# Up projections of a transformer layer computed in sets of four blocks by seven quarter products

## The reference

```python
# first layer, D_FF = 4096
h = rms_norm(x, norm_mlp[layer])
x = x + jnp.square(jax.nn.relu(h @ w_up[layer])) @ w_down[layer]

# two layers, two feed-forward parts each, D_FF_2 = 2816
def swiglu(h, w_gate, w_up, w_down):
    return (jax.nn.silu(h @ w_gate) * (h @ w_up)) @ w_down
mod = (c_act @ w_ada[l] + b_ada[l]).reshape(B, N_MOD, D_MODEL)
h = modulate(rms_norm_2(x, norm_gain[l, 0]), mod[:, 0], mod[:, 1])
x = x + 0.5 * mod[:, 2][:, None, :] * swiglu(h, ffn_w_gate[l, 0], ffn_w_up[l, 0], ffn_w_down[l, 0])
```

## Time and profile before

| | us |
|---|---|
| median of 3 runs | 3502.74 (3502.47 to 3504.43) |
| span of the profiled execution | 3498.8 |
| TensorE busy | 3407.7 (97%) |
| GpSimd busy | 2369.8 (68%) |
| VectorE busy | 1179.6 (34%) |
| ScalarE busy | 885.8 (25%) |

### The profile page before, as it was taken

How to read it: one execution, slowest core, us unless ns; L and a number is a source line. 1 busy time by engine, 2 the same in 40 slices (tenths; PEclk the granted TensorE clock), 3 DMA queues, 4 the chain that set the end, 5 groups by cost and what they waited for, 6 DMA issues and landing times.

```text
span 3498.8 us, 42521 instructions
## 1 busy us (share of the span) xinstructions
PE 3407.7 (97%) x17034; PEld 2738.7 (78%) x17034; DVE 1179.6 (34%) x2514; ACT 885.8 (25%) x1876; POOL 2369.8 (68%) x1242
## 2 busy tenths in 40 slices
PE   8888999999999999999999999999999999999999
PEld 6655777988898888667779888888887677798887
DVE  6554332433443234442223111332244422241111
ACT  2656551211120102354312000210012543221000
POOL 7515447787778776645677877687775546678775
PEclk9999999999999999999999999999999999999999
DMA  3222213444535442212232222254432122223222
GB/s 142 68 69 82 67 62 108 149 171 170 185 127 204 168 166 94 73 58 85 85 106 96 97 97 96 83 220 165 171 126 73 67 76 79 82 97 106 98 98 73
DMA packets 104773, 388.09 MB, mean 111 GB/s; under 512 B 12017, under 2 KB 12401, under 8 KB 98433
## 3 DMA queue, kind: packets, MB, share of 16 engines
q1 hardware_dynamic: 88272, 292.76, 24.4%
q10 hardware_dynamic: 16304, 92.62, 7.0%
HBM read 383.20 MB, written 2.13 MB: 110 GB/s over the span
## 4 chain that ended last, share of the span: by engine, by line
PE 92%; DVE 4%; ACT 3%; issue 1%; ACTq 0%; DVEq 0%
PE psum L1234 28%; PE psum L1236 27%; PE psum L1235 27%; PE psum L1307 2%; PE psum L1349 2%; PE psum L1324 2%; PE psum L1293 1%; DVE rs_t L1695 1%; ACT s_sb L1477 0%; DVE s_sb L1736 0%; ACT L1477 0%; ACT s_sb L1495 0%; PE psum L1407 0%; PE psum L1285 0%; DVE n_sum L1906 0%
## 5 line engine op out<-in xcount | busy, mean ns | idle before, releaser
L1202 POOL TENSOR_TENSOR w_hi<-raw,ones 128x1024 fp32r<-128x1024 f32 (+2 forms) x593 | 1041.3, 1756 | 990.4 <-PE psum L1236 981.2
L1205 POOL TENSOR_TENSOR w_lo<-raw,w_hi 128x1024 fp32r<-128x1024 f32 (+2 forms) x593 | 1315.1, 2218 | 46.5
L1234 PE MATMUL psum<-h_hi,w_hi 128*128 128x512 f32 (+2 forms) x2912 | 1143.4, 393 | 19.4 <-DVE r L1711 9.4
L1236 PE MATMUL psum<-h_hi,w_lo 128*128 128x512 f32 (+2 forms) x2912 | 1105.3, 380 | 0.0
L1235 PE MATMUL psum<-h_lo,w_hi 128*128 128x512 f32 (+2 forms) x2912 | 1104.8, 379 | 0.0
L1234 PEld LDWEIGHTS psum<-h_hi,w_hi 128*128 128x128 f32 (+1 forms) x2912 | 550.2, 189 | 156.6 <-issue 35.9
L1236 PEld LDWEIGHTS psum<-h_hi,w_lo 128*128 128x128 f32 (+1 forms) x2912 | 549.7, 189 | 106.6
L1235 PEld LDWEIGHTS psum<-h_lo,w_hi 128*128 128x128 f32 (+1 forms) x2912 | 550.9, 189 | 103.3 <-issue 9.0
L1234 PE MATMUL psum<-a_hi,w_hi 128*128 128x512 f32 (+1 forms) x1064 | 392.5, 369 | 0.0
L1235 PE MATMUL psum<-a_lo,w_hi 128*128 128x512 f32 (+1 forms) x1064 | 391.8, 368 | 0.0
L1236 PE MATMUL psum<-a_hi,w_lo 128*128 128x512 f32 (+1 forms) x1064 | 391.8, 368 | 0.0
(11 more groups left out here) (198 smaller groups left out, 3299.5 us busy)
## 6 DMA issues: line engine op xcount, KB each, us to landing
raw<-weights_dram SPq DMA_DIRECT2D x487, 512.0 KB, 3.3
ada_t<-ada_dram ACTq DMA_DIRECT2D x48, 1536.0 KB, 7.1
raw<-weights_dram SPq DMA_DIRECT2D x76, 256.0 KB, 2.6
raw<-weights_dram SPq DMA_DIRECT2D x32, 384.0 KB, 2.9
bias_t<-biases_dram ACTq DMA_DIRECT2D x36, 256.0 KB, 2.9
bias_t<-cum_dram ACTq DMA_DIRECT2D x16, 256.0 KB, 3.9
out_dram<-x SPq DMA_DIRECT2D x8, 256.0 KB, 2.1
raw<-weights_dram SPq DMA_DIRECT2D x4, 408.0 KB, 3.1
```

Of the source, the lines that this page charges most:

```text
L1202: nc.gpsimd.tensor_tensor(high, piece, ones[:, 0:1].to_broadcast([P, n]), ALU.mult)\
L1205: nc.gpsimd.tensor_tensor(w_lo[:, p % NR, 0:n], piece, high.bitcast(F32), ALU.subtract)\
L1234: mm(dst, lh, rh, start=first, stop=False)
L1236: return mm(dst, ll, rh, start=False, stop=last)
```

## The change

`ffn` and `mlp` no longer make all gates and ups as groups. The first four groups after each norm stay as they were (before it was three that were interleaved with the norm). All others come in sets of four groups, made by `new_set`: two pairs, "g" and "u" (for a feed-forward part two gate blocks and the two up blocks that belong to them; for the MLP four blocks). A pair is a product of 256 output features x 1024 features x 512 tokens. Each matrix is cut into 2x2 quarters, and the pair is made of seven quarter products P1 to P7 in place of eight, with sums of weight quarters and of activation quarters as operands. A quarter product is 4 chunks x 3 passes = 12 matmuls of 256 columns. The two pairs take turns: P1g, P1u, P2g, P2u, P6g, P6u, P5g, P5u, P7g, P7u, P4g, P4u, P3g, P3u. There are 47 sets: 7 in the MLP (1, 2, 2, 2 in its four parts) and 10 in each of the four feed-forward parts (3, 4, 3).

What comes with it:

- Operands. Each of the 14 products has its own place in the ring of six: half of the place is the high part, made by ACT as a copy of 128x512 (L1690), the other half is the low part, by GpSimd, for P3 by VectorE (L1995).
- Weight sums on VectorE, 8 per set, 128x512, SBUF to SBUF (L2006, L2008, L2009 are `first_sums`; L2017 is `last_sum`).
- Result sums. ACT copies P1, P6 and P5 out of PSUM (`keep`, L1701); VectorE adds (`combine`, L2024, L2028, L2033), 6 of 128x256 per set.
- Activation sums per norm: `quarter_sum` (4 instructions of 128x256), a high part on ACT and a low part on VectorE (128x1024, L1990) for each of 4 chunks. The normed value goes to SBUF (`n_out`) rather than to PSUM.
- Adaptation sums: 72 loads of 2 x 1024 columns, and c lies in SBUF (`c_t`) rather than in PSUM.

```diff
-ADA = 3
+ADA = 2
+SET_BANKS = (((0, 1), (2, 3)), ((6, 7), (5, 4)))
+PRODUCTS = ("P1", "P2", "P6", "P5", "P7", "P4", "P3")
...
+def with_operands():
...
+        while place < len(RING) and (place < NH or place - NH in free):
+            one = RING[place]
...
+            yield "operand", one
...
+    for what in PRODUCTS:
+        for p in pairs:
+            put("product", p.ops[what])
+            if what == "P1":
+                p.p1 = tick("copied")
+                put("keep", p, "P1")
+            elif what == "P2":
+                p.c11 = tick("combined")
+                put("c11", p)
...
+            elif what == "P3":
+                p.c12 = tick("combined")
+                put("c12", p)
+                result(p, 0)
...
+            def product(op):
+                pair, what, m = op.pair, op.what, op.pair.norm
+                E.wait_at(op.low)
...
+                elif what == "P6":
+                    E.wait_ge("copied", pair.p1)
+                elif what == "P5":
+                    E.wait_ge("combined", pair.c11)
...
+                    mm(dst, wh[:, w], hi, start=start, stop=False, skip_group_check=True)
+                    mm(dst, wh[:, w], lo, start=False, stop=False, skip_group_check=True)
+                    ins = mm(dst, wl[:, w], hi, start=False, stop=stop, skip_group_check=True)
+                ins.then_inc(sem["product_done"], 1)
...
+            def operand(op):
+                if op.low[0] == "low_dve":
+                    operand_low(op)
+                gate, up = SETS[op.pair.made // 8]
+                if (op.what, op.pair.side) == ("P2", 1):
+                    first_sums(gate)
+                elif (op.what, op.pair.side) == ("P6", 0):
+                    first_sums(up)
+                elif (op.what, op.pair.side) == ("P6", 1):
+                    last_sum(gate)
+                elif (op.what, op.pair.side) == ("P5", 0):
+                    last_sum(up)
...
-                    ins = v.tensor_tensor_reduce(out=part, in0=part, in1=c_bcast, scale=1.0, scalar=0.0, op0=ALU.mult,
+                    ins = v.tensor_tensor_reduce(out=part, in0=part, in1=c_t[:], scale=1.0, scalar=0.0, op0=ALU.mult,
```

429 lines of the change are left out of this document (359 added, 70 removed).

## The result

The changed kernel takes 3793.91 us (median of 4 runs, 3792.62 to 3797.42) against 3502.6 us for the kernel before (4 runs): ratio 1.0832, 95% interval [1.0817, 1.0848]. It is slower by 291 us. The forecast was 3640 and the range ended at 3720, so the sign was right and the size was not: the sum said +140, the profiled spans say 3795.6 - 3498.8 = +297.

A forecast was written before the change was run, and what follows sets the result against it. It took TensorE, busy for 97% of the span, as the bound; -76 + 1.5 + 73 + 48 + 40 + 44 + 10 = +140 us on the 3498.8 us span, with 3.9 around it, gave 3640 us, range 3560 to 3720.

The forecast's parts named there:

- TensorE's own work: All 47 sets: 168 matmuls of 256 columns take 20.2 us where 96 of 512 took 21.8; -76 us.
- From set to set: Feed-forward transitions with a set behind a set: 28 stalls of 2.6 us before P6g, +73 us (0 to 112).
- the walk: Step-by-step timing of one feed-forward transition: P6g waits for the P1g copy, at 28.5 rather than 25.9 us.
- the turns with GpSimd: VectorE's instructions with two SBUF inputs and GpSimd's exclude each other; without turns the transition walk ends at 25.8, no stall.
- Downs with sums: 51 downs carrying an adaptation sum: each loses 0.65 us once GpSimd's 2.7 us lead is gone; +10 us (0 to 33).
- The cycle: In downs with a sum, GpSimd's 4.3 us and two instructions' 2.4, in turns, take about 6.1 us against TensorE's 5.44.
- a first set behind downs finds operands and engines ready: Sets right behind downs: costed at nothing, as are last sets in front of downs.
- Adaptation sums in transitions: Feed-forward transitions holding adaptation sums: the P1g copy comes 3.5 us later per load; two layers +48 us (30 to 70).
- MLP: The MLP's 3 transitions, four products in place of two: P6g 10.1 us late, 13.5 with an adaptation sum; +40 us (20 to 50).
- Behind norms: First P6g behind a norm: stall 8 us at four norms, 11.5 at the MLP's, from activation sums on VectorE; +44 us.
- Norms' first groups: First groups at the 5 norms: no loss forecast beyond the fourth group in halves, which was +1.5 us.
- The rival of the shared path: VectorE and GpSimd's shared path is itself the bound, 22.3 us per set against TensorE's 20.2: 3740 us, chance 0.07.

The follow-up runs named there:

- Run 2: The changed kernel with GpSimd's low parts of the operands made over 16 of their 512 columns: 3627.17 us.
- run 1: The changed kernel with the first result of a set queued behind the next set's copy of P1 and its sum c11: 3749.08 us.
- Run 9: The kernel before with 30 idle stretches put into TensorE's queue in the two feed-forwards without sums, waiting for ScalarE's small copies: 3662.44 us (one run).
- run 3: The changed kernel with the adaptation's sums over 16 of 1024 columns, loads, places and waits kept: 3691.07 us.
- run 6: The changed kernel with no two sets adjacent (23 sets in place of 47, old-form groups between) and c back in PSUM: 3559.2 us.
- run 7: The kernel with sets apart, 23 sets, with the adaptation sums reading c from SBUF in place of PSUM, SiLU left out of them: 3629.66 us.
- run 8: The changed kernel with the activation's sums after a norm queued ahead of the first groups' last chunk: 3786.85 us.
- run 10: Against the changed kernel: 14 sets, only in feed-forwards, three first groups per norm, block sums spread over five groups, MLP and c as before: 3556.72 us.
- run 11: Ten sets, only in feed-forwards without adaptation sums, normalised activation through PSUM and made again for block sums, fourth group on bank 5: 3496.52 us.

## Why the prediction was wrong

- **TensorE's own work, -76.** Right: 20.2 us a set wherever nothing holds it.
- **From set to set, +73.** Place, releaser and size were right: 2.0 to 3.1 us before P6g, released by L1701, where the walk had 2.6. The 14 plain transitions cost 48 us, 13 of it at the lower clock: 2.5 us each without it. Run 2 agrees with the condition that the prediction named, the turns with GpSimd (though it cuts GpSimd's own time with them), and run 1 shows the line on ACT.
- **The missing term: the clock.** The prediction priced a stall at its length and closed with nothing on the clock, although it rested on matmuls at the upper level. Summed over all starts, the spacing of the lower level costs 74 us more in the changed kernel than before. Run 9 shows the price by itself: about 1.7 us more behind 18 of 19 idle stretches of 2.4 us or longer, next to none behind 9 of 10 below 2 us; in the changed kernel waits of 2.0 us mostly paid it and the four of 3.0 us did not. No row of before that the prediction showed follows an idle stretch of that kind. The trace of before has one, shown with run 9, which cost 2.0 us.
- **Downs with sums, +10, measured +67.** The cycle was right, 6.1 against 6.17 us. The step that failed is "a first set behind downs finds operands and engines ready ... I cost both at nothing": it looked at the set and not at the downs that its weight sums stand among. Three of them, 1.7 us each by turns, and a wait for GpSimd lie ahead of an addition to x in the feed-forwards' four rows, and VectorE has no lead left to cover them, because the loads are spread evenly over jobs, a set is one job in place of four groups, and so nearly each down carries two sums. Runs 3, 6 and 7 show the cause: with the sums cut, the feed-forwards' rows are at 43.3 us and the MLP's at 46.1; with 8 to 10 sums and c in PSUM all are at 43.3, and with c in SBUF at 48.3 to 53.2. The 2.5 us at the start of the MLP's rows, and of its row of four, were in no term: the prediction covered the last product's chain of a set (2.7 us) by six chunks, for a feed-forward set with two products; an MLP set has four.
- **Adaptation sums in transitions, +48.** 117 us in the 14 transitions of the feed-forwards with sums, less the 48 that the 14 plain ones cost: 69, of it 14 the clock's, so 55 by the prediction's way of counting. The last transition of each layer, said to cost about 4 us more than a plain one, costs 11 more: the walk left out the instructions that close the modulation, and the four sums took 2.3 us each.
- **MLP, +40.** 50, 8 of it clock: 42.
- **Behind norms, +44.** The stall before P6g was 8.6 to 9.5 us at four norms, where 8 was said, and 17.5 in the MLP, where 11.5 was said. The term was mis-sized, and its releaser was another: not the low part of the activation sums (L1990) but ACT's copy of P1g (L1701) once more, held up by those sums through their high part. In run 8 the block sums' place was worth 7 us.
- **Norms' first groups, 0, measured +27.** The step that failed is the list of instructions that the change turns into two-SBUF ones: "8 sums, 2 low parts and all adaptation sums". It left out the norm's low parts, 16 to a norm, whose input moved from PSUM to SBUF. In the changed kernel 10 of these 80 took 1.6 to 2.3 us in place of 0.48. Runs 10 and 11 show it together, though run 11 also leaves out four sets and moves the fourth group's bank: in both, every norm whose value stays in PSUM takes 18.0 us.
- **Slips in its sums** that move no term: 2 x (1.21 + 0.1) is 2.62 and not 2.65, 12 x 1.29 is 15.5 and not 15.4, and an overlap of 0.2 us for each of 22 instructions brings 22.3 to 17.9 and not 18.6.
- **The rival of the shared path,** 3740 us at 0.07, came nearest. Its sum, 22.3 us of turns to a set, is not what is seen (plain transitions of 22.8 to 23.8 with sets behind downs at 20.2 speak for the walk); but its sense, that the pair VectorE and GpSimd is the bound wherever two-SBUF work stands dense, holds in downs and norms.

The Trainium skill (GPSIMD Engine Reference, Key points) had named the contention. The trace agrees, and adds the price: a VectorE instruction waits out GpSimd's running one, and the other way round.

What stays open: what share of run 2's gain is GpSimd's own time, why the transitions of the feed-forwards with sums, other than the last of each layer, still cost 4.9 us with the sums cut, and what decides whether the clock falls behind a wait of 2 to 3 us.

## What to carry to other kernels

When an edit moves an operand from PSUM to SBUF, list every instruction that reads it, not only the new ones, and count VectorE's instructions with two operands in SBUF beside GpSimd's work: it is their density in the worst stretch that counts, not the total. Price an idle stretch of TensorE by its length plus what the clock may take behind it, here 1.5 to 3 us behind nearly every one of 3.7 us or longer, and read from the trace whether it did, since among those of 2 to 3 us some paid and some did not. A saving of 7.5% that leaves the feeding engines a lead of 9 us where they had 33 has to be placed where they have slack: here that was next to downs, and between groups of the old form, and it was worth 0.2%.
